# Sigmoids written as tanh, a second memory input split in place, and a new order of the side work in a two-block transformer kernel

## The chip, the cores and the metric

The kernel runs on one core of one Trainium2 chip. The metric is the device time of one execution in microseconds (us); lower is better. TensorE runs at one of two clock levels, 1.2 and 2.4 GHz; the profile prints the clock that was granted as a share of the higher one.

## The reference

512 tokens of width 1024 go through a chain of two blocks. All arrays are float32.

```python
# first block: layer A (mLSTM), then layer B (latent attention)
mem_n = rmsnorm(mem, mem_norm)                      # 256 memory tokens
mk, mv = memory_kv(mem_n, mem_w_kv[layer])          # once for each layer
# layer A
h = rmsnorm(x, norm_g)
qk, v, o, z, i_pre, f_pre, mq, mz = split_cols(h @ w_in, ...)
qk = silu(causal_conv(qk, conv_w, conv_b))
ht = rmsnorm(mlstm_chunkwise(q, k, v, i_pre + ig_b, f_pre + fg_b), h_g)
y_m = sigmoid(o) * ht * silu(z)                     # 4 heads of 256
y_mem = memory_attention(mq, mk, mv) * silu(mz)     # 4 heads of 128
x = x + concat(y_m, y_mem) @ w_out
# layer B: k, v from a latent of x, q from a latent, 8 heads of 192 with rope
y_b = chunk_causal_attention(q, k, v) * silu(z)
y_mem = memory_attention(mq, mk, mv) * silu(mz)
x = x + concat(y_b, y_mem) @ w_out
# second block, layer C
u, q, k, v, gate_logits = split(rms_norm(x, g_mix) @ w_in)
a = softmax(s[:, :, 0]) - lam * softmax(s[:, :, 1]) # differential attention, 4 heads
o = rms_norm(a @ v, g_subln) * (1 - lam_init)
mixed = concat(causal_multiscale_pool(u), o) * sigmoid(gate_logits)
x = x + mixed @ w_out
# layer D: cross attention to 256 tokens of mem_2, then the MLP
mem_n = rms_norm(mem_2, g_mem)
x = x + memory_cross_attention(rms_norm(x, g_cross), mem_n, w_cq, w_ckv, w_co)
x = x + square(relu(rms_norm(x, g_mlp) @ w_up)) @ w_down
return rms_norm(x, g_final)
```

## The kernel before

**Products.** Activations lie with features on the partitions. Each large product takes its weights in chunks of at most 512 columns by two tiles of 128 rows. A chunk is loaded (SP) into one of two raw slots, ScalarE writes its rounded high part (L1505), VectorE the low part (L1862), and TensorE adds three products, high by high, high by low and low by high (L1205 to L1207 with the activations stationary, L1210 to L1212 with the weights stationary). There are three slots for split chunks. The products are called after their outputs, in this order: mqA, mk0, mv0, mzA, then for each head of layer A qkA, ozA and vA (one for two heads), outA0 and outA1; qlB, ckvB, mk1, mv1; zB0, kvB0, quB0, mqB, kvB1, quB1, mzB0, mzB1, kvB2, quB2, zB1, kvB3, quB3, zB2, zB3, outB0, outB1; kC, qC, vC, gC4, uC, gC0, outC0, outC1; ckD0, ckD1, cqD0, cqD1, cvD0, cvD1, outD0, outD1; and up and dn of the MLP. gC4 and gC0 are the gate logits of layer C, for the attention half and for the pooling half; ckD is the keys of the cross attention, which read mem_2.

**Side work.** Everything else is cut into small steps: one score tile of an attention head (`msc`, `asc`, `dsc`, `csc`), the transposes of its probabilities (`mtp`, `atp`, `dtp`; L1168), the product with the values (`mval`, `aval`, `dval`; L1410), norms (`nsq`, `nsum`, `ndiag`, `nrow`), the gates of the mLSTM (`gateP`, `gateA`, `gateT`), the preparation of layer B's queries and keys (`prep0` to `prep6`). A unit of the differential attention is one head with one block of 128 queries: `dsc` (two score tiles, L1397, with a mask, L1184), its softmaxes, `dtp` and `dval`. At a unit's score tile VectorE takes the maximum, ScalarE the exponential, VectorE the sum's reciprocal and the scaling.

**Order.** `order_of_work()` writes one list of steps, and the program of every engine follows that list, so each engine's queue is fixed when the kernel is built. Two lanes hold side steps. After each row of a product (one tile of 128 contraction rows, L1186) `step()` takes the next group from a lane if its conditions have been put into the list and if at least `lag` ns of a planner's clock have gone by since the last group of that lane. Where a product needs a result that is still in a lane, `need()` and `force()` put the steps of the lane there one after the other, with no row of a product between them. The closing steps of the differential attention's heads (`dhs`, `dhr`, `dho`: the norm, a transpose, and the multiplication by the gate) wait in the lane for gC0's gate, and the units behind them in the same lane with them.

**ScalarE's functions.** Sigmoid and Exp belong to different table sets, and a set is loaded (ACT_TABLE_LOAD) where the function changes. SiLU is sigmoid on ScalarE (L1610) and a multiplication on VectorE (L1862); in the convolution of layer A the multiplication is GpSimd's (`csilu`, L2417).

**Memory of layer D.** mem_2 is loaded after outC0, turned (scaled by its gain and split into high and low parts) during outC1, and its norm follows after outC1. The evictions of a product that reads a normed input scale by the norm's row, so they need `nrow` first; ckD0's evictions are put behind `nrow m2`, and with it the norm's matmuls stand in TensorE's queue between the last row of ckD0 and the first of ckD1.

## Time and profile before

| what | value |
| --- | --- |
| device time, median of 3 | 1767.71 us (1767.44 to 1769.67) |
| the profiled execution's own time | 1770.57 us |
| its span in the trace | 1768.8 us |
| TensorE busy | 1649.4 us, 93% of the span |
| VectorE, ScalarE, GpSimd busy | 911.1, 730.8, 133.4 us |
| mean granted clock | 0.952 |

TensorE has little idle time in sum, so the table is read for two quantities: where its 7% of idle time lies, and where its granted clock is under 1.00. The rows by stage are further down. In the trace layer A's first head (qkA0) begins at 91.2 us, mk1 at 530.2, mzB0 at 638.2, quB2 at 695.7, zB1 at 733.7, outB0 at 837.9, kC at 928.8, gC4 at 1001.2, the last row of gC0 ends at 1079.5, outC0's first tile follows at 1106.0, outC1 begins at 1178.5, ckD0 at 1200.9, ckD1 at 1227.6 and the MLP at 1391.3.

### The profile page before, as it was taken

The numbers are of one execution on the slowest core, as the hardware profiler recorded it, in microseconds if no ns is written. First come the engines' busy times: TensorE is split into PE (matmuls) and PEld (weight loads), VectorE is DVE, ScalarE is ACT, GpSimd is POOL, SyncE is SP. The second block draws the span as 40 slices with busy tenths as digits, with TensorE's granted clock in tenths as the row PEclk, the third lists the DMA queues.
The fourth block names the chain that finished last, engine by engine and source line by source line (L and its number), as shares of the span: only waits on it lengthen the run. The fifth ranks groups of instructions, "written<-read, shape, count | busy, mean of one in ns | idle before, by whom it ended". The sixth has DMA issues, their size and how long they took to land.

```text
span 1768.8 us, 19339 instructions
## 1 busy us (share of the span) xinstructions
PE 1649.4 (93%) x7194; PEld 1276.1 (72%) x7194; DVE 911.1 (52%) x1853; ACT 730.8 (41%) x1618; POOL 133.4 (8%) x106
## 2 busy tenths in 40 slices
PE   7997999999998997888999998887999999999997
PEld 5755687777886866465678775566877788888885
DVE  6346465656466445456446556464454543434342
ACT  5534433334356566456333343343333342424241
POOL 3101010101110000000001000012000200000001
PEclk9998999999999999799999997697999999999997
DMA  5512212313324211111123221022332333333331
GB/s 173 142 48 60 60 50 82 96 52 115 113 84 121 67 43 44 32 36 60 60 84 96 84 72 59 3 85 81 105 97 73 95 95 95 96 95 96 95 96 48
DMA packets 90109, 140.99 MB, mean 80 GB/s; under 512 B 7456, under 2 KB 37536, under 8 KB 90016
## 3 DMA queue, kind: packets, MB, share of 16 engines
q1 hardware_dynamic: 89296, 139.02, 26.1%
q8 instruction: 57, 0.93, 0.2%
q10 hardware_dynamic: 720, 0.74, 0.1%
q14 instruction: 36, 0.29, 0.1%
HBM read 137.65 MB, written 2.10 MB: 79 GB/s over the span
## 4 chain that ended last, share of the span: by engine, by line
PE 73%; DVE 12%; ACT 7%; issue 4%; DMA 2%; POOL 1%; ACTq 0%; POOLq 0%; DVEq 0%; SPq 0%
PE banks L1205 15%; PE banks L1207 15%; PE banks L1206 15%; PE banks L1210 5%; PE banks L1212 5%; PE banks L1211 5%; DVE sb_arena L1862 3%; DVE sb_w_split L1862 3%; PE banks L1168 2%; DVE sb_arena L1871 2%; PE banks L1397 1%; ACT sb_w_split L1505 1%; ACT sb_junk L1473 1%; DMA sb_raw<-in_mem_w_kv 1%; ACT sb_arena L1642 1%
## 5 line engine op out<-in xcount | busy, mean ns | idle before, releaser
L1862 DVE TENSOR_TENSOR sb_w_split<-sb_raw,sb_w_split 128x512 fp32r<-128x512 f32 (+3 forms) x530 | 335.8, 676 | 363.3 <-ACT sb_w_split L1505 361.7
L1505 ACT ACTIVATE sb_w_split<-sb_raw 128x512 fp32r<-128x512 f32 (+3 forms) x530 | 287.8, 593 | 427.3 <-PE banks L1207 327.8
L1205 PE MATMUL banks<-sb_actA,sb_w_split 128*128 128x512 f32 x672 | 273.6, 407 | 2.5 <-ACT sb_arena L1560 1.1
L1207 PE MATMUL banks<-sb_actA,sb_w_split 128*128 128x512 f32 x672 | 263.4, 392 | 0.0
L1206 PE MATMUL banks<-sb_actA,sb_w_split 128*128 128x512 f32 x672 | 262.9, 391 | 0.0
L1205 PE MATMUL banks<-sb_actB,sb_w_split 128*128 128x512 f32 (+1 forms) x640 | 253.9, 397 | 7.9 <-DVE sb_actB L1862 4.4
L1206 PE MATMUL banks<-sb_actB,sb_w_split 128*128 128x512 f32 (+1 forms) x640 | 249.0, 389 | 0.0
L1207 PE MATMUL banks<-sb_actB,sb_w_split 128*128 128x512 f32 (+1 forms) x640 | 248.8, 389 | 0.0
L1210 PE MATMUL banks<-sb_w_split,sb_actA 128*128 128x512 f32 (+1 forms) x384 | 155.7, 406 | 12.9 <-DVE sb_w_split L1862 8.7
L1212 PE MATMUL banks<-sb_w_split,sb_actA 128*128 128x512 f32 (+1 forms) x384 | 150.7, 393 | 0.0
L1211 PE MATMUL banks<-sb_w_split,sb_actA 128*128 128x512 f32 (+1 forms) x384 | 150.4, 392 | 0.0
L1205 PEld LDWEIGHTS banks<-sb_actA,sb_w_split 128*128 128x128 f32 x672 | 127.1, 189 | 31.6 <-issue 5.5
L1205 PEld LDWEIGHTS banks<-sb_actB,sb_w_split 128*128 128x128 f32 x640 | 123.3, 193 | 36.3 <-issue 5.5
L1207 PEld LDWEIGHTS banks<-sb_actA,sb_w_split 128*128 128x128 f32 x672 | 126.8, 189 | 27.5
L1206 PEld LDWEIGHTS banks<-sb_actA,sb_w_split 128*128 128x128 f32 x672 | 127.2, 189 | 25.8 <-issue 1.5
L1207 PEld LDWEIGHTS banks<-sb_actB,sb_w_split 128*128 128x128 f32 x640 | 122.8, 192 | 27.1
L1206 PEld LDWEIGHTS banks<-sb_actB,sb_w_split 128*128 128x128 f32 x640 | 123.2, 192 | 26.3 <-issue 0.7
L1168 PE MATMUL banks<-sb_cons,sb_arena 128*128 128x128 f32 x460 | 83.6, 293 | 39.9 <-DVE sb_arena L1862 13.2
L2400 POOL TENSOR_TENSOR sb_arena<-sb_arena 128x512 f32<-128x512 f32 x44 | 65.4, 1488 | 716.7 <-ACT sb_arena L1546 713.9
L1168 PEld LDWEIGHTS banks<-sb_cons,sb_arena 128*128 128x128 f32 x460 | 59.1, 150 | 61.8 <-issue 17.1
L2391 POOL TENSOR_TENSOR sb_small<-sb_small,sb_cons 128x4 f32<-128x4 f32 (+3 forms) x30 | 41.7, 1389 | 785.2 <-DVE sb_small L1868 731.1
L1642 ACT ACTIVATE sb_arena<-banks,sb_small 128x256 f32<-128x256 f32 (+2 forms) x80 | 45.4, 567 | 128.9 <-DVE sb_small L1865 128.8
(176 smaller groups left out, 2167.7 us busy)
## 6 DMA issues: line engine op xcount, KB each, us to landing
sb_raw<-in_a_w_in SPq DMA_DIRECT2D x66, 256.0 KB, 3.0
sb_raw<-in_w_up SPq DMA_DIRECT2D x32, 512.0 KB, 3.7
sb_raw<-in_w_down SPq DMA_DIRECT2D x32, 512.0 KB, 3.8
sb_raw<-in_w_in SPq DMA_DIRECT2D x24, 512.0 KB, 3.6
sb_raw<-in_mem_w_kv SPq DMA_DIRECT2D x16, 512.0 KB, 3.9
sb_raw<-in_w_ckv SPq DMA_DIRECT2D x16, 512.0 KB, 3.9
sb_raw<-in_a_w_in SPq DMA_DIRECT2D x15, 512.0 KB, 3.9
sb_raw<-in_a_w_out SPq DMA_DIRECT2D x12, 512.0 KB, 3.9
```

The costliest lines, as they stand in the source:

```text
L1168: t = pe.op.transpose(v.ps[0:rows, place.bank, n * P:(n + 1) * P], block, v.ident)
L1205: pe.op.matmul(out, hi[:, cs], x.hi(k), start=i == 0, stop=False)
L1206: pe.op.matmul(out, hi[:, cs], x.lo(k), start=False, stop=False)
L1207: t = pe.op.matmul(out, lo[:, cs], x.hi(k), start=False, stop=last_i)
L1210: pe.op.matmul(out, x.hi(k)[:, cs], hi, start=i == 0, stop=False)
L1211: pe.op.matmul(out, x.hi(k)[:, cs], lo, start=False, stop=False)
L1212: t = pe.op.matmul(out, x.lo(k)[:, cs], hi, start=False, stop=last_i)
L1505: act.op.activation(hi[:, cs], raw[:, cs], ACT.Copy).then_inc(act.mark(m("w_hi"), 2 * n + part + 1), 1)
L1642: act.op.activation(prob, src, ACT.Exp, bias=v.soft("mx", step, 1), scale=scale, accum_out=v.soft("sm", step, 1)).then_inc(act.mark(empty, ...
L1862: dve.op.tensor_tensor(out, a, b, op).then_inc(dve.mark(*mark) if mark else dve.tick(), 1)
L2391: pool.op.tensor_tensor(v.stat(root, n), v.stat(mean, n), v.con("minus_half", 0, n), ALU.pow).then_inc(m.at("rstd", step)[0], 1)
L2400: pool.op.tensor_tensor(total, total, v.square_of(norm, n)[1], ALU.add).then_inc(signal, 1)
```

## The change

It does seven things.

1. Sigmoid becomes Tanh of half the argument, sigmoid(x) = (tanh(x/2) + 1)/2. The +1 goes into the multiplication that follows, which becomes a scalar_tensor_tensor (`fused`), and the factor 1/2 into constants further on. In `csilu` the multiplication by (tanh + 1) becomes two instructions of GpSimd, a multiplication and an addition. The program has 5 table loads in place of 36.
2. The ones are a constant instead of a memset by GpSimd, and `ndiag` and `nrow` are groups of their own with a lag of 2600 each, in place of one with 4500.
3. mem_2 is loaded after outB1 into places of the second activation buffer that are free then, turned in place, and its norm stands in kC and qC; between ckD0 and ckD1 there is none.
4. A row of a product is issued in parts, one for each 128-column output, and side steps may stand between the parts; a lane that is forced lets the other lane advance too.
5. The differential attention has its transposes two units behind the scores instead of one, a third buffer of probabilities, a lag of 4000 for 4600, and its closing steps wait for the gate of gC4 instead of gC0's.
6. Layer B is in another order, below.
7. In layer A `gateT` has a lag of 14000 for 4000 and the memory rounds 8000 for 4400.

```diff
@@ class Plan: force, product
             self.take(lane)
+            self.advance(1 - lane)
...
                 self.put(("mm", name, i), banks)
-                self.clock += row_ns(name)
+                for j in range(n_out(name)):
+                    self.put(("rows", name, i, j))
+                    self.clock += row_ns(name) / n_out(name)
+                    if j < n_out(name) - 1:
+                        self.advance((i * n_out(name) + j) % 2)
@@ order_of_work: scales, layer A
-            p.side(lane, (), ("ndiag", norm), ("nrow", norm), lag=4500)
+            p.side(lane, (), ("ndiag", norm), lag=2600)
+            p.side(lane, (), ("nrow", norm), lag=2600)
...
-    p.side(1, (), ("gateT",), lag=4000)
+    p.side(1, (), ("gateT",), lag=14000)
...
-           [("hnscale", "mqA"), ("silu", "mzA", 3), ("hnt", "mk0", 3)])
+           [("hnscale", "mqA"), ("silu", "mzA", 3), ("hnt", "mk0", 3)], lag=8000)
@@ layer B
     p.product("mk1")
     head_norm(0, "mk1", MT, False)
+    p.product("mqB")
+    head_norm(0, "mqB", TT, True)
     p.product("mv1")
...
-    gated("zB0")
-    p.need(("kpe",))
-    latents(0)
-    p.product("mqB")
-    mla(0)
-    head_norm(1, "mqB", TT, True)
     mem_b(0)
     mem_b(2)
-    latents(1)
     p.need(("nrow", "b"))
     gated("mzB0")
     gated("mzB1")
-    mla(2)
+    p.need(("kpe",))
+    latents(0)
+    gated("zB0")
+    for n in range(4):
+        mla(2 * n)
+    latents(1)
+    p.need(("mtp", "B", 3, 3))
+    gated("zB1")
     latents(2)
-    p.need(("mval", "B", 3))
-    gated("zB1")
-    mla(4)
-    latents(3)
     p.need(("ysplit", "yB", 1))
     gated("zB2")
+    latents(3)
     p.need(("ysplit", "yB", 3))
     gated("zB3")
-    mla(6)
@@ layer C: mem_2
     p.put(("enter", "outB1"))
+    p.put(("load_mem2",))
     p.put(("late",))
     scales(0, "c", after=[("sqp", "c", 7)])
+    for n in range(4):
+        p.soon.append(squares("m2", n) + [("turn", "m2T", 2 * n), ("turn", "m2T", 2 * n + 1)])
     p.product("kC", [("nsum", "c")])
+    scales(1, "m2", after=[("sqp", "m2", 3)])
@@ layer C: differential attention
-    for n, u in enumerate(units + [None] * 5):
+    for n in range(len(units) + 6):
...
-                after = [("gateG", "gC0")]
+                after = [("gateG", "gC4")]
...
-        if before is not None:
-            group.append(("dtp", *before))
-            turned = before
-        before = u
-        p.side(0, after, *group, lag=4600)
+        if 2 <= n < len(units) + 2:
+            turned = units[n - 2]
+            group.append(("dtp", *turned))
+        p.side(0, after, *group, lag=4000)
...
-    p.put(("load_mem2",))
-    for k in range(KD):
-        p.soon.append([("turn", "m2T", k)])
     p.product("outC1")
     p.put(("enter", "outC1"))
-    for n in range(4):
-        p.soon.append(squares("m2", n))
-    scales(1, "m2", after=[("sqp", "m2", 3)])
     scales(0, "d", after=[("sqp", "d", 7)])
-    p.product("ckD0", [("nrow", "m2")])
+    p.product("ckD0")
@@ scalar_program: silu
-            act.op.activation(sg, v.out_of(name, j), ACT.Sigmoid)...
+            act.op.activation(sg, v.out_of(name, j), ACT.Tanh, scale=0.5)...
@@ vector_program: silu
-            tensor(o, o, v.sigA[:, j % 2, :] if name == "mzA" else v.sigB[:, 0, :], ALU.mult, *m.at("silu", step))
+            fused(o, v.sigA[:, j % 2, :] if name == "mzA" else v.sigB[:, 0, :], 1.0, ALU.add, o, ALU.mult,
+                  *m.at("silu", step))
@@ gpsimd_program: csilu
-                pool.op.tensor_tensor(v.qkT[:, n, :], v.conv[:, n, :], v.u_pad[:, n, CONV_W - 1:CONV_W - 1 + SEQ],
-                                      ALU.mult).then_inc(m("qk"), 1)
+                t = v.u_pad[:, n, CONV_W - 1:CONV_W - 1 + SEQ]
+                pool.op.tensor_tensor(t, t, v.conv[:, n, :], ALU.mult).then_inc(pool.tick(), 1)
+                pool.settle()
+                pool.op.tensor_tensor(v.qkT[:, n, :], t, v.conv[:, n, :], ALU.add).then_inc(m("qk"), 1)
```

Line numbers move with the edits: the instructions of a product row are L1205 to L1207 before and L1213 to L1215 now, the score tiles L1397 and L1404, the transposes L1168 and L1176.

**TensorE's queue where gC0 ends and outC0 begins, before.** The first row is the last of gC0. Score tiles (L1397), masks (L1184), values (L1410) and transposes (L1168) of the differential attention follow, and L1420, which is a product of the pooling.

```order
L1207 MATMUL banks<-sb_actA,sb_w_split 128x512
L1420 MATMUL banks<-sb_arena 128x512 [waits dma_pool_w,pooled]
L1410 MATMUL banks<-sb_arena 128x128 [waits empty4,empty5]
L1410 MATMUL banks<-sb_arena 128x128 x3
L1397 MATMUL banks<-sb_arena 128x256 [waits empty6]
L1184 MATMUL banks<-sb_masks 128x128
L1397 MATMUL banks<-sb_arena 128x256
L1184 MATMUL banks<-sb_masks 128x128
L1168 MATMUL banks<-sb_cons,sb_arena 128x128 [waits empty5,prob]
L1410 MATMUL banks<-sb_arena 128x128 [waits empty5,empty6]
L1397 MATMUL banks<-sb_arena 128x384 [waits empty4]
L1184 MATMUL banks<-sb_masks 128x128
```

Behind these rows stand 22 more of the same kinds; only then comes the first row of outC0 (`L1205 MATMUL banks<-sb_actB,sb_w_split`). A second such stretch stands behind the first row of outC0's first tile.

**TensorE's queue in a product of layer C, now.** The place is inside one of the products gC4, uC and gC0.

```order
L1213 MATMUL banks<-sb_actA,sb_w_split 128x512 [waits empty0,w_lo]
L1214 MATMUL banks<-sb_actA,sb_w_split 128x512
L1215 MATMUL banks<-sb_actA,sb_w_split 128x512
L1417 MATMUL banks<-sb_arena 128x128 [waits empty5,empty6]
L1404 MATMUL banks<-sb_arena 128x512 [waits empty4]
L1192 MATMUL banks<-sb_masks 128x128
L1404 MATMUL banks<-sb_arena 128x512
L1192 MATMUL banks<-sb_masks 128x128
L1176 MATMUL banks<-sb_cons,sb_arena 128x128 [waits empty6,prob]
L1176 MATMUL banks<-sb_cons,sb_arena 128x128
L1213 MATMUL banks<-sb_actA,sb_w_split 128x512 [waits empty1]
L1214 MATMUL banks<-sb_actA,sb_w_split 128x512
```

The score tiles and transposes of a unit now stand between the three matmuls of one output part and those of the next.

**ScalarE's queue in layer B, before.** L1610 is the sigmoid of a gate, L1642 the exponential of a memory-attention score, L1652 and L1740 copies out of PSUM, L1505 the weight split.

```order
L1610 ACT_TABLE_LOAD [waits silu]
L1610 ACTIVATE sb_cons<-sb_arena 128x512 [waits empty0]
L1740 ACTIVATE sb_arena<-banks 128x512 [waits full7]
L1642 ACT_TABLE_LOAD [waits neg]
L1642 ACTIVATE sb_arena,sb_small<-banks,sb_small 128x256 [waits full6]
L1652 ACTIVATE sb_actB_plain<-banks 128x2x128 [waits full4]
L1740 ACTIVATE sb_arena<-banks 128x512 [waits full7]
L1505 ACTIVATE sb_w_split<-sb_raw 128x192 [waits full1,dma_raw1]
L1505 ACTIVATE sb_w_split<-sb_raw 128x192
L1610 ACT_TABLE_LOAD [waits silu]
L1610 ACTIVATE sb_cons<-sb_arena 128x512 [waits empty1]
L1642 ACT_TABLE_LOAD [waits neg]
```

**ScalarE's queue at a like place, now.** L1617 is the tanh of the gate, L1649 the exponential, L1659 the copy, L1512 the weight split.

```order
L1512 ACTIVATE sb_w_split<-sb_raw 128x384 [waits chunk,dma_raw0]
L1512 ACTIVATE sb_w_split<-sb_raw 128x384
L1649 ACTIVATE sb_arena,sb_small<-banks,sb_small 128x256 [waits neg,full4]
L1659 ACTIVATE sb_actB_plain<-banks 128x2x128 [waits full5]
L1617 ACTIVATE sb_cons<-sb_arena 128x512 [waits silu,empty0]
L1512 ACTIVATE sb_w_split<-sb_raw 128x192 [waits full1,dma_raw1]
L1512 ACTIVATE sb_w_split<-sb_raw 128x192
L1649 ACTIVATE sb_arena,sb_small<-banks,sb_small 128x256 [waits neg,full6]
L1659 ACTIVATE sb_actB_plain<-banks 128x2x128 [waits full4]
L1617 ACTIVATE sb_cons<-sb_arena 128x512 [waits silu,empty1]
L1649 ACTIVATE sb_arena,sb_small<-banks,sb_small 128x256 [waits neg,full5]
L1659 ACTIVATE sb_actB_plain<-banks 128x2x128 [waits full6]
```

The four table loads are gone; the gate's function and the exponential follow each other without one.

**TensorE's queue between ckD0 and ckD1, before.** The first row is the last of ckD0, the next three are the norm of mem_2 (L1237 sums the squares, L1246 spreads the scale over the partitions), and then comes ckD1.

```order
L1207 MATMUL banks<-sb_actB,sb_w_split 128x256
L1237 MATMUL banks<-sb_cons,sb_arena 128x1 [waits sq_sum,empty7]
L1237 MATMUL banks<-sb_cons,sb_arena 128x1 x3
L1246 MATMUL banks<-sb_arena 128x256 [waits empty7,diag,ones]
L1205 MATMUL banks<-sb_actB,sb_w_split 128x256 [waits empty0,w_lo]
```

**The same place, now.** The first row is the last of ckD0, and ckD1 follows without a norm.

```order
L1215 MATMUL banks<-sb_actB,sb_w_split 128x256
L1213 MATMUL banks<-sb_actB,sb_w_split 128x256 [waits empty0,w_lo]
L1214 MATMUL banks<-sb_actB,sb_w_split 128x256
L1215 MATMUL banks<-sb_actB,sb_w_split 128x256
```

The norm of mem_2 stands between rows of a product of layer C instead:

```order
L1220 MATMUL banks<-sb_w_split,sb_actA 128x512
L1245 MATMUL banks<-sb_cons,sb_actB_plain 128x1 [waits sq_sum]
L1245 MATMUL banks<-sb_cons,sb_actB_plain 128x1 x3
L1218 MATMUL banks<-sb_w_split,sb_actA 128x512 [waits w_lo]
```

The summing matmuls (now L1245) wait for `sq_sum`, GpSimd's sum of the squares, as before, but with product rows of layer C around them.

## Rows read from the trace of the kernel before

**Rows 1.** The page: busy time by engine, and the granted clock in 40 slices.
```profile
PE 1649.4 (93%) x7194; PEld 1276.1 (72%) x7194; DVE 911.1 (52%) x1853; ACT 730.8 (41%) x1618; POOL 133.4 (8%) x106
...
PEclk9998999999999999799999997697999999999997
```

**Rows 2.** Windows by stage: length, busy time of each engine, granted clock, DMA.
```profile
0.00:66.40 66.40, 53.02 (x211) 41.73 (x211) 37.62 (x60) 35.07 (x64) 17.79 (x22) 0.95 0.57 177
91.00:208.80 117.80, 104.57 (x396) 71.48 (x394) 62.65 (x126) 47.16 (x97) 8.77 (x5) 0.93 0.20 58
540.60:838.00 297.40, 258.56 (x1120) 188.19 (x1119) 155.43 (x414) 174.01 (x484) 19.10 (x10) 0.92 0.18 54
...
1001.20:1079.50 78.30, 76.78 (x344) 60.10 (x342) 44.64 (x101) 29.17 (x64) 0.00 (x0) 1.00 0.26 80
1079.50:1178.50 99.00, 81.28 (x285) 51.48 (x284) 48.60 (x128) 34.91 (x104) 4.03 (x4) 0.72 0.07 22
1200.90:1244.30 43.40, 31.19 (x213) 29.76 (x212) 21.46 (x43) 17.19 (x33) 12.44 (x11) 0.76 0.30 85
```

**Rows 3.** The same view, of short stretches inside those stages.
```profile
34.40:39.10 4.70, 1.17 (x4) 0.58 (x3) 3.34 (x7) 1.47 (x4) 1.41 (x2) 0.81 0.03 12
130.20:143.80 13.60, 7.83 (x25) 5.71 (x26) 10.96 (x20) 3.39 (x8) 0.00 (x0) 0.62 0.14 40
152.70:178.10 25.40, 18.23 (x65) 13.31 (x65) 13.83 (x28) 14.36 (x27) 5.87 (x4) 0.87 0.23 62
705.80:734.00 28.20, 19.36 (x50) 9.53 (x47) 11.45 (x38) 11.10 (x39) 0.00 (x0) 0.69 0.03 10
755.50:770.00 14.50, 8.06 (x31) 5.97 (x29) 8.11 (x21) 5.87 (x12) 0.00 (x0) 0.76 0.13 36
1079.50:1106.00 26.50, 19.84 (x62) 10.54 (x60) 14.01 (x38) 11.03 (x31) 1.01 (x1) 0.61 0.07 22
1110.30:1136.00 25.70, 20.50 (x63) 11.10 (x62) 12.12 (x34) 7.93 (x28) 1.01 (x1) 0.61 0.00 1
```

**Rows 4.** VectorE's timeline in one unit of the differential attention.
```profile
1027.66 0.69 DVE L2287 TENSOR_REDUCE sb_small<-banks 128x1 f32<-128x512 f32 x1
...
1031.35 0.17 DVE L2292 RECIPROCAL sb_small<-sb_small 128x2 f32<-128x2 f32 x1 [1.58 <-ACT sb_arena L1776]
...
1031.81 0.75 DVE L1871 SCALAR_TENSOR_TENSOR sb_arena<-sb_arena,sb_small 128x512 f32<-128x512 f32 x1
1032.48 0.68 DVE L1862 TENSOR_TENSOR sb_arena<-banks,sb_arena 128x512 f32<-128x512 f32 x1
```

**Rows 5.** TensorE's waits: us in total, times, longest.
```profile
PE banks L1168 <- DVE sb_arena L1862: 13.2, 4, 6.4
...
PE banks L1237 <- POOL sb_arena L2400: 9.4, 1, 9.4
...
PE banks L1210 <- ACT sb_arena L1560: 3.5, 2, 3.1
```

**Rows 6.** The page: a DMA issue, its KB and us to landing.
```profile
sb_raw<-in_w_in SPq DMA_DIRECT2D x24, 512.0 KB, 3.6
```

**Rows 7.** ScalarE by line: busy us, mean ns, idle before.
```profile
L1642 ACT ACT_TABLE_LOAD x12 | 15.4, 1283 | 34.6 <-DVE sb_small L1865 34.6
```

**Rows 8.** ScalarE's timeline round one table load: start, length.
```profile
91.05 1.28 ACT L1610 ACT_TABLE_LOAD   x1
92.34 0.63 ACT L1610 ACTIVATE sb_arena<-sb_x_res 128x512 f32<-128x512 f32 x1
```

**Rows 9.** VectorE's and GpSimd's timelines in one stretch of the convolution.
```profile
255.38 2.33 DVE L1871 SCALAR_TENSOR_TENSOR sb_arena<-sb_arena,sb_cols 128x512 f32<-128x512 f32 x3
...
258.20 4.29 DVE L1871 SCALAR_TENSOR_TENSOR sb_arena<-sb_arena,sb_cols 128x512 f32<-128x512 f32 x3
...
258.15 2.99 POOL L2417 TENSOR_TENSOR sb_arena<-sb_arena 128x512 f32<-128x512 f32 x2 [17.26 <-ACT sb_arena L1658]
```

173 lines of the change are left out of this document (95 added, 78 removed).

## The prediction

> **What bounds the kernel now.** I read the page first [rows 1]: TensorE is busy for 93% of the span and no other engine for more than 52%, so the end is set by TensorE's work plus whatever interrupts it. The strip of granted clocks says the rest: most slices are at 9, and 6 or 7 in a few places. A time over stretches therefore has two losses: idle time, and busy time at a lower clock. For a stretch of length L with busy time B and granted clock c, I count loss = (L - B) + (1 - c) B; the second part is what the same work would have saved at full clock.
>
> The windows by stage [rows 2] give these losses: 13.4 + 2.7 = 16.0 us up to 66.4; 13.2 + 7.3 = 20.5 in layer A's first head (91.0 to 208.8); 38.8 + 20.7 = 59.5 from mk1 to the end of layer B's attention (540.6 to 838.0); 1.5 + 0 in gC4, uC and gC0; 17.7 + 22.8 = 40.5 in outC0 and the stretch ahead of it (1079.5 to 1178.5); 12.2 + 7.5 = 19.7 round ckD0 (1200.9 to 1244.3). Together 156.2 us. The matmuls themselves are not made fewer by the change, so a gain has to come out of these 156.2 us.
>
> Inside the stages I looked for knots [rows 3]. Loss by the same formula: 3.8 (34.4), 8.8 (130.2), 9.5 (152.7), 14.8 (705.8), 8.4 (755.5), 14.4 (1079.5), 13.2 (1110.3). In the last two, TensorE executes some 62 instructions in 26 us, at 0.61 of the clock, with VectorE busy for half of the time: score, softmax and transpose follow each other, nobody has other work to put between. The reader is to see there the forced steps that the queue listings show: no product rows, so each engine waits for the other. The granted clock is 1.00 in the 78 us before, with 98% busy, and falls where TensorE comes to be busy for 75% (19.84 of 26.5).
>
> **The change, part by part.**
>
> *Layer C (28 us).* The closing steps wait for gC4's gate instead of gC0's, so the lane is no longer blocked through uC and gC0, and the units of the two forced stretches go between product rows. Is there room? The work moved is 19.84 x 0.61 + 20.50 x 0.61 = 24.6 us of TensorE at full clock and 14.0 + 12.1 = 26.1 us of VectorE [rows 3]. gC4 to gC0 now have 44.6 us of VectorE in 78.3 [rows 2]; with the moved work it is 70.8 in 102.9, or 69%. So it fits on average. The latency of one unit is 1032.56 - 1027.66 = 4.9 us from the first maximum to the scaled probabilities [rows 4], and with the transposes two units behind the scores, at least one product row stands between. I take both forced losses as gone, 14.4 + 13.2 = 27.6, and leave the other 12.9 us of the 40.5. Bounds: 41 (all of it), and 12 if the in-order queue of VectorE paces each unit (below).
>
> *Layer B (40 us).* Of 59.5 us, the block of forced memory-attention steps between quB2 and zB1 is 14.8 [rows 3], and it goes: the memory units come earlier, beside mzB0 to zB0. What stays, by my count: mk1 is now followed by mqB, whose first row waits for the same ScalarE copies, 3.1 of the 3.5 us [rows 5]; two of the four waits for `prep6` (L1168 behind L1862, 13.2 in total, longest 6.4 [rows 5]) remain forced, at the ends of zB0 and zB2, since latents(1) and the queries of the last heads need them: 2 x 6 = 12; and gaps of about 5 us where softmaxes pace. That is 20, so 59.5 - 20 = 39.5. Bounds: 20, if only the forced block (14.8) and a little of the rest (5) goes; 60, if all goes. VectorE has 155.4 us of work in 297.4, 52% [rows 2], so it has the room.
>
> *Layer A (14 us).* 20.5 us of loss, of which 8.8 lie at 130.2 (the gates of the mLSTM, forced, at 0.62 of the clock) and 9.5 at 152.7 [rows 3]. The memory rounds with a lag of 8000 leave room in VectorE's queue, and the gate chain starts earlier relative to the convolutions. I take the first entirely and half of the second: 8.8 + 4.8 = 13.6. Bounds 5 and 20.
>
> *Start (4.5 us).* `nrow a` moves into mqA instead of following it, which is the knot at 34.4 [rows 3]: 3.8; with no memset to wait for, some 0.7 more. The loads of the first weights stay. Bounds 0 and 7.
>
> *Entry of layer D (14 us).* The norm of mem_2 no longer stands between ckD0 and ckD1. It ended a wait of 9.4 us for GpSimd [rows 5], and the stretch's low clock (7.5 of the 19.7) came with it. Where the stall goes: in kC and qC the same sum by GpSimd has product rows round it, and nobody needs the row before ckD0's evictions. What is late next I can't read off a row; I leave the other 5.7 us of the stretch in place. mem_2's two loads now stand in SP's queue ahead of weights of kC; a chunk of w_in lands 3.6 us after its issue [rows 6], so the delay lies between 0 and 3.6, and I take 0, as the raw slots are filled ahead. Bounds 8 and 18.
>
> *Tanh.* 31 table loads of 1283 ns leave ScalarE, 39.8 us [rows 7]. ScalarE isn't the bound, so that is worth nothing by itself; only the 12 loads ahead of an exponential (15.4 us) stand in the chain score, maximum, exponential, transpose. Where TensorE waits for that chain they are inside the losses above, and I add nothing; if they came on top, 15.4 more. The next ACTIVATE starts 0.01 us after a load ends [rows 8]. The Trainium skill (ScalarE: Activation LUTs, What ACT_TABLE_LOAD costs) puts a drain of about 1380 ns on top of each load; this row shows none, and by the page that upper bound would be 12 x 2.66 = 32 us. The fused form costs 0.75 us for 0.68 [rows 4], for some fifty instructions 4 us of VectorE, hidden under product rows.
>
> *The convolution's second GpSimd instruction (costs 4 us).* 16 more instructions of 1.49 us (2.99 for two) [rows 9], 24 us of GpSimd, which is idle otherwise. But three fused operations of VectorE take 2.33 us alone and 4.29 us beside 2.99 us of GpSimd's: 0.65 us lost for each us. So 24 x 0.65 = 15.6 us of VectorE at most, in layer A, where its share is 53% [rows 2]; a quarter on the path is 4. Bounds 0 and 15.6. The Trainium skill (SBUF — State Buffer, Who interferes with whom) says that a VectorE instruction with two SBUF inputs and a GpSimd instruction that reads SBUF exclude each other for their whole length; that speaks against this edit, and by it the bound would be 24 us and not 15.6. The row shows a delay of two thirds.
>
> **Sum.** 28 + 40 + 14 + 4.5 + 14 - 4 = 96.5 us. The profiled execution took 1770.6 us (1.8 over its span) and is 2.9 over the median of 1767.7. So 1770.6 - 96.5 - 2.9 = 1671.
>
> **The rivals.** A measurement of this kernel can tell about 0.2% (3.5 us) from no change.
>
> *Main case*, all as summed: 1671, own range 1652 to 1690, chance 0.55.
>
> *VectorE's queue paces (0.20).* The queue is in order, so a unit's maximum may stand behind a weight split that waits for ScalarE, and the next weights' split behind the unit's reciprocal. For: in the unit shown, 1.6 of 4.9 us are one wait for ScalarE's exponential [rows 4]. Against: the full clock in gC4 to gC0 with units already between rows [rows 2]. Then layer B gives 20 and layer C 12: 1671 + 20 + 16 = 1707.
>
> *Nothing left (0.14).* The split of product rows lets every unit hide, B gives 60 and C 41: 1671 - 20 - 13 = 1638. For: VectorE's 52% and 69%. Against: the prep6 waits are forced still.
>
> *GpSimd's lock on the path (0.05).* All 15.6 us: 1671 + 11 = 1682.
>
> *The clock stays low (0.06), the other side.* If spread units make TensorE as little busy in gC4 to gC0 as in the forced stretch (75% busy, clock 0.61), a us of product work takes 1 / (0.75 x 0.61) = 2.19 us, 1.19 more. With C's 28 lost, 68.5 us of gain are left, and 68.5 / 1.19 = 58 us of the 78 decide: beyond, the kernel is slower. For all 78: 1671 + 28 + 93 = 1792; for half, 1745. For: spread work makes small gaps everywhere, where now they are in two places. Against: from 540.6 to 838.0, with units all through and 87% busy, the mean was still 0.92 [rows 2].
>
> **How the numbers follow.** The range 1640 to 1708 runs from the case with nothing left to that of VectorE's queue; outside lie the low clock (0.06), half of the best case and a tail of the queue's, 0.18 in all. Faster by over 0.2%: 0.94. Slower: 0.05, the low clock over 58 us. Within: 0.01.
>
> **What would show it.** In the new trace: no stretch without product rows near 1010 us and 990 us of the new span (the old 1079 and 1110), and the clock strip at 9 there; layer B's loss near 20, with two waits of L1176 for VectorE of 5 to 6 us; no wait of TensorE for GpSimd at ckD1; 5 table loads; VectorE's convolution rows longer beside GpSimd's. The prediction is wrong if the forced stretches turn into many waits of 0.5 to 2 us for VectorE or ScalarE in B and C, or if the clock strip shows more than four slices under 9.

## The result and the profile after

The changed kernel takes 1716.7 us (median of 4, 1714.8 to 1722.0) against 1767.7 us: ratio 0.971, 95% interval 0.969 to 0.974. It is faster, but by 51 us, about half of the 96.5 that the prediction had, and it lies 9 us outside the predicted range. The profiled execution took 1714.8 us, its span is 1713.0.

The page of the changed kernel, its engines and its strip of granted clocks (answers to [rows 1]):

```profile
PE 1611.0 (94%) x7194; PEld 1258.9 (73%) x7194; DVE 921.0 (54%) x1856; ACT 691.6 (40%) x1587; POOL 149.6 (9%) x115
...
PEclk9998999999999999999999999899999999999998
```

The slices at 7 and 6 are gone, and three slices are under 9, fewer than the prediction's sign of being wrong (more than four). In this respect the mechanism came out as forecast. Where the time came from is to be read by stage. The windows of the changed kernel, cut at the first rows of qkA0, qkA1, mk1, outB0, kC, gC4, outC1, ckD0, cqD0, up00 and dn31 (columns as in [rows 2]: length, busy time of each engine, clock, DMA):

```profile
89.20:190.80 101.60, 95.71 (x368) 67.17 (x369) 58.07 (x108) 34.10 (x71) 12.31 (x9) 0.95 0.22 63
190.80:411.70 220.90, 213.45 (x949) 163.75 (x947) 137.08 (x264) 68.47 (x146) 34.19 (x27) 1.00 0.21 63
524.20:818.20 294.00, 259.03 (x1161) 191.31 (x1161) 161.16 (x426) 164.23 (x497) 20.11 (x11) 0.97 0.20 60
818.20:905.60 87.40, 85.46 (x372) 64.14 (x373) 42.99 (x84) 32.90 (x68) 4.26 (x3) 1.00 0.23 76
905.60:983.40 77.80, 73.37 (x341) 59.27 (x340) 53.15 (x109) 32.07 (x60) 12.01 (x9) 1.00 0.34 102
983.40:1144.30 160.90, 147.25 (x626) 105.20 (x625) 93.52 (x228) 59.44 (x163) 4.03 (x4) 0.94 0.18 53
1166.00:1196.40 30.40, 26.76 (x204) 25.89 (x204) 21.02 (x35) 13.60 (x24) 7.42 (x5) 0.94 0.39 123
1342.40:1670.60 328.20, 328.20 (x1451) 271.55 (x1450) 147.13 (x223) 114.77 (x193) 7.45 (x5) 1.00 0.31 97
```

The kernel before, cut at the same products, where [rows 2] had other cuts:

```profile
208.80:415.60 206.80, 205.96 (x926) 160.53 (x924) 128.53 (x250) 73.14 (x141) 21.53 (x15) 1.00 0.24 69
530.20:837.90 307.70, 268.67 (x1161) 195.90 (x1161) 162.16 (x430) 182.44 (x511) 20.11 (x11) 0.92 0.19 56
837.90:928.80 90.90, 87.95 (x372) 64.95 (x373) 42.78 (x80) 34.17 (x69) 4.26 (x3) 1.00 0.24 76
928.80:1001.20 72.40, 71.56 (x332) 58.17 (x330) 45.89 (x97) 26.27 (x46) 7.44 (x6) 1.00 0.33 95
1001.20:1178.50 177.30, 158.06 (x627) 111.57 (x625) 93.24 (x228) 64.07 (x167) 4.03 (x4) 0.85 0.16 48
...
1391.30:1724.70 333.40, 333.13 (x1451) 271.30 (x1450) 147.23 (x223) 114.71 (x193) 7.60 (x6) 1.00 0.32 95
```

| stretch | before | after | saved | forecast |
| --- | --- | --- | --- | --- |
| mqA to qkA0 | 83.3 | 80.6 | 2.7 | 4.5 |
| layer A, head 0 (qkA0 to qkA1) | 117.6 | 101.6 | 16.0 | 14, less 4 for GpSimd |
| layer A, heads 1 to 3 | 206.8 | 220.9 | -14.1 | 0 |
| mk1 to outB0 | 307.7 | 294.0 | 13.7 | 40 |
| outB0 to kC | 90.9 | 87.4 | 3.5 | 0 |
| kC to gC4 | 72.4 | 77.8 | -5.4 | 0 |
| gC4 to outC1 | 177.3 | 160.9 | 16.4 | 28 |
| ckD0 to cqD0 | 43.4 | 30.4 | 13.0 | 14 |
| up00 to dn31 (MLP) | 333.4 | 328.2 | 5.2 | 0 |

The lengths are differences of the starts of the products in the two traces. The rows add up to 51.0 us; the stretches between them that are left out give 3.8 more, and the start and the end 1.0. So the traces lie 55.8 us apart, 5 more than the medians: the profiled execution of the kernel before was slower than its median, and that of the changed kernel faster. Four lines have a forecast of 0 and moved all the same: heads 1 to 3, outB0 to kC, kC to gC4, and the MLP, in which no step was changed.

By loss (idle plus the share of busy time that the clock took), mk1 to outB0 went from 39.0 + 21.5 to 35.0 + 7.8 us, and gC4 to outC1 from 19.2 + 23.7 to 13.7 + 8.8. (The latter is the place of both forced stretches.) So in layer B only 4.0 us of idle time went, and 13.7 came from the clock, less 4 us that TensorE's work (busy time by clock) grew. The prediction had layer B's loss near 20 us; it is 42.8. TensorE's waits in the changed kernel, for mk1 to outB0 (us in total, times, longest):

```profile
PE banks L1218 <- DVE sb_arena L1875: 6.6, 2, 4.7
PE banks L1176 <- DVE sb_arena L1875: 5.7, 4, 3.5
PE banks L1176 <- ACT sb_arena L1750: 4.4, 2, 3.4
PE banks L1213 <- DVE sb_arena L1875: 4.1, 2, 2.4
PE banks L1218 <- ACT sb_arena L1567: 3.6, 2, 3.2
PE banks L1218 <- ACT sb_arena L1591: 3.0, 2, 1.5
```

L1213 and L1218 are the first matmuls of product rows, L1176 is a transpose. The prediction kept two waits of L1176 for VectorE, of 6 us each; there are four, 5.7 us together. The rows of L1213 and L1218 are waits of a product's first row for work of VectorE or ScalarE, and only one of them (L1567, 3.2 us behind mk1) was in its count.

In the stretch from gC4 to outC1 the other sign of being wrong did show: the forced stretches turned in part into 8 waits of 0.5 to 2 us, 11.3 us together. Before there were 6 such waits, 7.8 us, beside 5 longer ones of 12.1 us.

### The profile page after: what moved, and what is told of

Its sections match the earlier page's. It is cut to its first block, busy times and chain, and to the rows that moved or that the text cites. A ratio compares the mean times of both kernels' runs of the same rounds, so it can differ in the third digit from the quotient of the medians.

```text
span 1713.0 us, 19330 instructions
## 1 busy us (share of the span) xinstructions
PE 1611.0 (94%) x7194; PEld 1258.9 (73%) x7194; DVE 921.0 (54%) x1856; ACT 691.6 (40%) x1587; POOL 149.6 (9%) x115
## 3 DMA queue, kind: packets, MB, share of 16 engines
q1 hardware_dynamic: 89296, 139.02, 26.7%
## 4 chain that ended last, share of the span: by engine, by line
PE 71%; DVE 15%; ACT 7%; issue 4%; DMA 3%; POOL 0%; SPq 0%; ACTq 0%; DVEq 0%; POOLq 0%
PE banks L1213 15%; PE banks L1215 15%; PE banks L1214 15%; PE banks L1218 4%; PE banks L1220 4%; PE banks L1219 4%; DVE sb_w_split L1875 4%; DVE sb_arena L1875 3%; DVE sb_arena L1884 3%; PE banks L1176 2%; ACT sb_junk L1480 2%; ACT sb_w_split L1512 1%; PE banks L1336 1%; DVE sb_arena L1878 1%; PE banks L1404 1%
## 5 line engine op out<-in xcount | busy, mean ns | idle before, releaser
L1875 DVE TENSOR_TENSOR sb_w_split<-sb_raw,sb_w_split 128x512 fp32r<-128x512 f32 (+4 forms) x530 | 342.0, 687 | 368.2 <-ACT sb_w_split L1512 367.1
L1512 ACT ACTIVATE sb_w_split<-sb_raw 128x512 fp32r<-128x512 f32 (+4 forms) x530 | 288.0, 593 | 439.1 <-PE banks L1215 323.5
L1213 PE MATMUL banks<-sb_actA,sb_w_split 128*128 128x512 f32 x672 | 279.4, 416 | 6.6 <-ACT sb_arena L1567 2.3
L1215 PE MATMUL banks<-sb_actA,sb_w_split 128*128 128x512 f32 x672 | 264.7, 394 | 0.0
L1214 PE MATMUL banks<-sb_actA,sb_w_split 128*128 128x512 f32 x672 | 264.5, 394 | 0.0
L1213 PE MATMUL banks<-sb_actB,sb_w_split 128*128 128x512 f32 (+1 forms) x640 | 249.0, 389 | 8.5 <-DVE sb_arena L1875 3.9
L1215 PE MATMUL banks<-sb_actB,sb_w_split 128*128 128x512 f32 (+1 forms) x640 | 243.7, 381 | 0.0
L1214 PE MATMUL banks<-sb_actB,sb_w_split 128*128 128x512 f32 (+1 forms) x640 | 243.6, 381 | 0.0
L1218 PE MATMUL banks<-sb_w_split,sb_actA 128*128 128x512 f32 (+1 forms) x384 | 156.1, 406 | 23.8 <-DVE sb_w_split L1875 9.1
L1213 PEld LDWEIGHTS banks<-sb_actA,sb_w_split 128*128 128x128 f32 x672 | 128.1, 191 | 37.8 <-issue 11.6
L1215 PEld LDWEIGHTS banks<-sb_actA,sb_w_split 128*128 128x128 f32 x672 | 127.7, 190 | 28.1
L1213 PEld LDWEIGHTS banks<-sb_actB,sb_w_split 128*128 128x128 f32 x640 | 121.4, 190 | 34.2 <-issue 10.7
L1214 PEld LDWEIGHTS banks<-sb_actB,sb_w_split 128*128 128x128 f32 x640 | 121.5, 190 | 23.1 <-issue 1.4
L1215 PEld LDWEIGHTS banks<-sb_actB,sb_w_split 128*128 128x128 f32 x640 | 121.4, 190 | 22.9
L2423 POOL TENSOR_TENSOR sb_arena<-sb_arena 128x512 f32<-128x512 f32 x41 | 61.6, 1501 | 705.9 <-ACT sb_arena L1553 703.3
L1649 ACT ACTIVATE sb_arena<-banks,sb_small 128x256 f32<-128x256 f32 (+2 forms) x80 | 45.4, 568 | 169.0 <-DVE sb_small L1878 169.0
L1218 PEld LDWEIGHTS banks<-sb_w_split,sb_actA 128*128 128x128 f32 x384 | 74.1, 193 | 41.2 <-issue 16.0
L1176 PE MATMUL banks<-sb_cons,sb_arena 128*128 128x128 f32 x460 | 80.8, 285 | 24.8 <-DVE sb_arena L1875 11.4
```

The costliest lines, as they stand in the source:

```text
L1176: t = pe.op.transpose(v.ps[0:rows, place.bank, n * P:(n + 1) * P], block, v.ident)
L1213: pe.op.matmul(out, hi[:, cs], x.hi(k), start=i == 0, stop=False)
L1214: pe.op.matmul(out, hi[:, cs], x.lo(k), start=False, stop=False)
L1215: t = pe.op.matmul(out, lo[:, cs], x.hi(k), start=False, stop=last_i)
L1218: pe.op.matmul(out, x.hi(k)[:, cs], hi, start=i == 0, stop=False)
L1512: act.op.activation(hi[:, cs], raw[:, cs], ACT.Copy).then_inc(act.mark(m("w_hi"), 2 * n + part + 1), 1)
```

## The experiments

All are compared with runs of the kernel before on the same chip, whose median lay between 1766.6 and 1767.2 us. Where a stretch is compared with the changed kernel's, its scatter has to be known: the same instructions took between 290.7 and 294.4 us from mk1 to outB0, between 158.0 and 164.9 from gC4 to outC1 and between 77.8 and 81.5 from kC to gC4 in the profiles of kernels whose code there is identical. Much of this goes with the granted clock (below). The experiments are spread over four chips, and where one is compared with another on a different chip (12, 14 and 17 with 11), a difference of a few us is weaker than its digits look.

**1. The place of actB.** The changed kernel also allocates the second activation buffer, actB, right behind actA, which the list of the change doesn't name. Here it goes back behind the other buffers:

```diff
         sb("actA", [P, 2, KD, SEQ], F32R)
-        with nc.sbuf_tensor("sb_actB", [P, 2, 12, SEQ], F32R) as both:
-            mem["actB"] = both
-        sb("actB_plain", [P, 2, 12, SEQ])
...
         sb("junk", [P, 512])
+        with nc.sbuf_tensor("sb_actB", [P, 2, 12, SEQ], F32R) as both:
+            mem["actB"] = both
+        sb("actB_plain", [P, 2, 12, SEQ])
```

> The changed kernel with one edit: the second activation buffer (actB) is allocated last again, as before, instead of right behind actA; orders, functions and steps stay. In the changed kernel each product that reads actB takes 21.8 us where it took 22.4, and those of 12 rows 32.6 where they took 33.6, and no step of theirs was changed. Theory one, the place of the buffer sets the length of its matmuls: the MLP goes back from 350.2 to 356 us, outA1 and outB1 to 33.6, and the kernel loses about 12 us, to some 1729. Rival, the place is nothing and the shorter products come from the new order of loads and splits: the time stays at 1717 within 3 us.

Measured: 1716.2 us (1711.8 to 1722.0), ratio 0.972 (0.969 to 0.974), and the MLP (up00 to dn31) 328.3 us. Theory one fell as it stood, and the rival's number held; its explanation did not, as the next two show.

**2. The same move in the kernel before.**

> The kernel before with that edit alone, the other way: actB allocated right behind actA. Theory one: the MLP falls from 356 to 350 us and the kernel from 1768 to about 1756. Rival: 1768 within 3 us.

Measured: 1757.3 us, ratio 0.995 (0.993 to 0.997): 9.4 us faster, as theory one had it. The windows from mk1 to outB0 and, further on, of the MLP:

```profile
526.60:831.40 304.80, 266.17 (x1160) 194.56 (x1161) 161.75 (x430) 182.42 (x511) 20.11 (x11) 0.93 0.20 57
...
1383.10:1711.80 328.70, 328.43 (x1451) 271.44 (x1450) 147.04 (x223) 114.68 (x193) 7.61 (x6) 1.00 0.32 96
```

So the place does count in the kernel before and not in the changed one. What differs is where actB begins when it stands last: the changed kernel's constants are 816 columns wide (the 128 columns of ones) against 689. So in the changed kernel actB begins at a multiple of 128 bytes in either place.

**3. Only the start of actB in the kernel before.**

```diff
-CONSTS = [..., ("minus_half", 16), ("ones", 1)]
+CONSTS = [..., ("minus_half", 16), ("ones", 1), ("spare", 15)]
```

> The kernel before with 15 unused columns added to its constants, and nothing else: every buffer that is allocated behind them moves up, and the second activation buffer (actB) begins at a multiple of 64 bytes instead of 32 bytes past one. Putting actB back behind the others in the changed kernel left its products at 21.8 us, and there too it begins at a multiple of 64 bytes, since the changed kernel's constants are wider. Theory one, that start is what counts: each product that reads actB falls from 22.4 to 21.8 us, the MLP from 356 to 350 and the kernel from 1767 to 1755 to 1758, as with actB moved forward. Rival, the neighbour or the bank of memory counts: 1767 within 3 us.

Measured: 1760.0 us, ratio 0.995 (0.993 to 0.997), 6.6 us faster, with no instruction changed. The MLP's window:

```profile
1385.00:1715.40 330.40, 330.13 (x1451) 271.53 (x1450) 147.22 (x223) 114.77 (x193) 7.60 (x6) 1.00 0.32 96
```

That is between the two others: 333.4, 330.4, 328.7. By the buffers' sizes, each rounded up to 32 bytes, actB begins 32, 64 and 0 bytes past a multiple of 128. The time falls short of theory one's 1755 to 1758. The products say the same as the windows: in the MLP each two down products, which read actB (192 matmuls), take 44.8, 44.0 and 43.5 us in these three, and the products of the same length that read actA take 43.5 or 43.6 in all of them. Between experiment 2 and the kernel before, actB alone changes its remainder, and experiment 1 shows that its place is nothing otherwise; a multiple of 128 is best of the three. The middle value is less sure: in experiment 3 the arena and the other buffers behind the constants move by 32 bytes too.

**4. The arena's start in the changed kernel** (one spare column; the arena then begins at a multiple of 128 bytes instead of 96 past one).

> The changed kernel with one unused column more in its constants, so that the arena, which holds nearly all of the small buffers, begins at a multiple of 128 bytes instead of 32 bytes before one, as it did in the kernel before; actB keeps its place. Theory one, as for actB, TensorE reads the arena's operands faster: matmuls on the arena are some 1000 of 7194 at about 7 ns each, so 3 to 8 us less, to about 1711. Rival, only operands of large products show it and the arena's place is nothing: 1717 within 3 us.

Measured: 1719.8 us (1711.4 to 1724.4), ratio 0.974 (0.972 to 0.977). No gain: the rival holds, though the four runs lie 13 us apart. The effect is seen for actB's products only.

**5. Sigmoid back in the changed kernel.**

```diff
-ACT.Tanh
+ACT.Sigmoid
```

> The changed kernel with Sigmoid in place of Tanh in every such ScalarE instruction, all else the same (the output is not the reference's, since the arithmetic round it is still that for tanh). It brings back 36 table loads, 41 in place of 5, and nothing else. Theory one, ScalarE has slack and only loads ahead of an exponential or an eviction on which TensorE waits count: 36 loads of 1.28 us are 46 us of ScalarE, and the kernel loses 5 to 15 us, to 1722 to 1732. Rival, the loads were worth nearly all that the change brought: the kernel loses 30 to 46 us, to about 1750 to 1763. Second rival, nothing: within 3 us of 1717.

Measured: 1740.5 us, ratio 0.985 (0.984 to 0.987), 24 us slower than the changed kernel. That is above theory one's 5 to 15 and below the rival's 30: neither number held. Its windows for head 0 and for mk1 to outB0:

```profile
87.50:196.40 108.90, 95.66 (x370) 67.13 (x370) 57.66 (x108) 42.69 (x78) 12.29 (x9) 0.92 0.20 58
...
535.80:841.50 305.70, 263.81 (x1160) 194.04 (x1160) 160.61 (x426) 184.70 (x513) 20.12 (x11) 0.94 0.20 57
```

In the second, ScalarE has 20.5 us more (184.7 for 164.2) and the stretch is 11.7 us longer, though ScalarE is busy for 60% of it. Layer A's heads 0 to 3 together are 13.3 us longer.

**6. Tanh in the kernel before**, the same edit the other way (the output is not the reference's).

> The kernel before with Tanh in place of Sigmoid as the function of each such ScalarE instruction and no other edit (its argument isn't halved and nothing is added, so the output is not the reference's): 5 table loads instead of 36, in the old order. Theory one, the loads cost about as much in the old order as in the new one, where putting them back cost 24 us: 1767 falls to 1740 to 1748. Rival, the old order's forced stretches hide or repeat the loads differently: under 12 us of gain, over 1755. Second rival, all of the change's gain but the place of actB: under 1735.

Measured: 1755.5 us, ratio 0.993 (0.992 to 0.995), 11.1 us faster, which is the rival's number (the two profiled executions lie 16 us apart). Its window from mk1 to outB0:

```profile
527.70:822.00 294.30, 260.96 (x1161) 192.09 (x1161) 162.45 (x430) 164.47 (x497) 20.11 (x11) 0.94 0.20 59
```

294.3 us, in the old order, with the forced block still in it (26.5 us without a product row): the table loads alone bring all that the whole change brought there (294.0). Of the 13.4 us, 5.7 are idle time and 5.8 the clock. The loads are worth 11 us in the old order and 24 in the new one; the rest of the difference lies mostly in layer A (3.1 us there in the old order, 13.3 in the new). Experiments 2 and 5 say the same from the other side: with sigmoid the stretch takes 304.8 us in the old order with actB moved, and 305.7 in the new one.

**7. Layer B in the old order, all else changed.**

> The changed kernel with layer B in the old order of products and lanes (zB0, kvB0, quB0, mqB and so on, and the forced memory-attention steps between quB2 and zB1), all other edits kept, tanh among them. With Sigmoid in place of Tanh the new layer B took 305.7 us against 307.7 in the kernel before, with tanh 294.0. Theory one, the new order is worth little and the tables carried layer B's gain: the stretch from mk1 to outB0 stays at 294 within 5 us and the kernel at 1717 within 6. Rival, as predicted, the order is worth the 14.8 us of the forced block and more: 15 to 30 us slower.

Measured: 1715.9 us, ratio 0.971 (0.969 to 0.973). The windows from mk1 to outB0 and on to kC:

```profile
527.30:821.20 293.90, 260.85 (x1168) 192.03 (x1169) 163.49 (x432) 164.82 (x499) 20.10 (x11) 0.96 0.20 59
821.20:906.10 84.90, 84.26 (x364) 63.60 (x365) 41.38 (x78) 31.96 (x66) 4.26 (x3) 1.00 0.25 81
```

Theory one holds: the new order is worth nothing. The forced block is still there, without a product row, and costs 9.5 us of idle time and 2.8 by the clock:

```profile
707.40:728.90 21.50, 11.99 (x37) 5.91 (x36) 6.84 (x24) 12.74 (x47) 1.64 (x1) 0.77 0.05 13
```

In the new order the longest stretch without a product row is 8.9 us, and yet idle time from mk1 to outB0 is 35.0 us without the block and 33.0 with it. The old order here has the old lag of the memory rounds (2400 ns for 2800) and the old condition ahead of kvB3 as well.

**8. and 9. Less work for VectorE or for ScalarE in layer B.** VectorE's edit; ScalarE's puts the same two lines ahead of its own part of the split.

```diff
+                if name in SHORT:
+                    cs = slice(part * half, part * half + 64)
```

> The changed kernel with VectorE's part of the weight split cut to 64 columns of each half in layer B's products (mk1 to zB3), so that it leaves out most of the low parts there (the output is not the reference's); each such instruction goes from about 0.7 to about 0.2 us, and some 120 of them save 50 to 60 of VectorE's 161 us in the 294 us of the stretch. Theory one, VectorE's queue is late there, since evictions and softmax steps stand behind splits: the stretch falls by 10 us or more, the kernel to 1707 or less. Rival, what is left are latencies of chains over several engines and forced steps, which VectorE's load does not change: under 5 us.

> The changed kernel with ScalarE's part of the weight split cut to 64 columns of each half in layer B's products (most of the high parts are left out, so the output is not the reference's); some 120 instructions fall from 0.6 to about 0.2 us and save some 45 to 50 of ScalarE's 164 us in the stretch of 294. The same cut on VectorE gave 6.2 us there. Theory one, ScalarE's queue is what lets TensorE wait in layer B, as the table loads (11 to 15 us of its time, 12 to 13 us of the stretch) say: the stretch falls by 12 us or more, the kernel to 1705 or less. Rival, the rest are chains of latencies and forced steps: under 6 us.

Measured: 1714.0 us (ratio 0.970, 0.968 to 0.972) with VectorE's splits cut, 1717.7 us (0.972, 0.970 to 0.975) with ScalarE's. The windows from mk1 to outB0, first VectorE's cut:

```profile
526.40:814.20 287.80, 256.47 (x1160) 190.30 (x1160) 138.56 (x425) 164.09 (x497) 20.10 (x11) 0.97 0.21 61
```

then ScalarE's:

```profile
525.00:813.90 288.90, 256.78 (x1163) 190.16 (x1161) 160.94 (x426) 143.91 (x497) 20.10 (x11) 0.97 0.21 61
```

VectorE's cut takes 22.6 us off VectorE, ScalarE's 20.3 off ScalarE (under half of what was expected of either), and the stretch falls by some 2 to 6 us from its 290.7 to 294.4. Idle time stays at 31.3 and 32.1. The rivals hold: the weight splits of either engine are a small part of what TensorE waits for. In the changed kernel's stretch TensorE waits once for a split:

```profile
PE banks L1218 <- DVE sb_w_split L1875: 0.2, 1, 0.2
```

That 20 us of table loads were worth 12 and 20 us of splits about 4 is no contradiction: a split is mostly done ahead, while the load in front of an exponential itself waits for the softmax's maximum ([rows 7]: ScalarE idles ahead of it). So ScalarE doesn't use its idle time for the load, and each of those stands whole in the chain. This reading is argued from the queue and the waits; no run moved the loads alone to other places.

**10. Side steps between whole rows only, everywhere.**

```diff
-                    if j < n_out(name) - 1:
-                        self.advance((i * n_out(name) + j) % 2)
```

> The changed kernel with no side step between the parts of a product row, so that side steps stand only between whole rows, as before (three matmuls for each of the outputs, then side steps); all other edits stay. Theory one, finer places for side steps gain a few us of waits and cost TensorE about as much in exposed weight loads (its work, busy time by clock, is 4 us more in layer B and 4 in layer C than before): within 5 us of 1717. Rival, the fine places carry the gain of layers B and C: 15 us or more slower, to over 1730. Second rival, they cost more than they bring: under 1712.

Measured: 1719.0 us, ratio 0.972 (0.971 to 0.974), as theory one had it. The windows from mk1 to outB0, outB0 to kC and, further on, gC4 to outC1:

```profile
523.50:804.60 281.10, 248.69 (x1123) 186.20 (x1124) 157.37 (x414) 158.70 (x485) 20.10 (x11) 0.96 0.22 63
804.60:917.10 112.50, 102.79 (x410) 73.29 (x411) 48.18 (x96) 37.76 (x80) 4.25 (x3) 0.92 0.18 57
...
992.10:1145.90 153.80, 144.42 (x628) 105.72 (x627) 92.33 (x228) 58.90 (x163) 4.40 (x4) 0.94 0.18 55
```

Layer B moves work into outB0 and loses 12 us in the two stretches together (393.6 us for 381.4); layer C gains 7, and kC to gC4 2.8. The small sum hides two effects of opposite sign. The old order with whole rows and tanh took 385.3 us in the same two stretches (experiment 6), so the new order seems to need the finer places only to break even.

**11. Whole rows from kC on only.**

```diff
-                    if j < n_out(name) - 1:
+                    if j < n_out(name) - 1 and self.fine:
...
     p.put(("enter", "outB1"))
+    p.fine = False
```

> The changed kernel with side steps between the parts of a product row up to outB1 only, and from kC on between whole rows. Without them anywhere, layers C's stretch (kC to outC1) fell from 238.7 to 228.8 us, and the stretch from mk1 to kC rose from 381.4 to 393.6. Theory one, these are two separate effects: the kernel gains 8 to 10 us, to about 1708. Rival, layer C's 10 us are noise of the clock or of how layer B leaves off: within 3 us of 1717.

Measured: 1706.7 us (1703.6 to 1706.9), ratio 0.965 (0.964 to 0.967). It is the fastest kernel of the study, 10 us faster than the changed one, as theory one had it. The window from gC4 to outC1:

```profile
982.10:1133.60 151.50, 141.02 (x626) 102.19 (x625) 92.10 (x228) 58.86 (x163) 4.40 (x4) 0.98 0.19 56
```

TensorE's work is the same (138 us by the clock). Idle time is 10.5 us and the clock 0.98, against 13.7 us and 0.94, so 3 of the 9.4 us are idle time and 6 the clock. The stretch took 151.1, 152.0 and 150.0 us in experiments 14, 17 and 18, which share nearly all of this code.

**12. A lag of 5200 for layer C's units on top of that.**

> The last but one kernel's edit (whole rows from kC on) with a lag of 5200 instead of 4000 for the units of the differential attention, which puts 5, 6 and 5 units into gC4, uC and gC0 instead of 6, 8 and 2. In the run with whole rows uC took 67.5 us and gC0 23.3. Theory one, uC is overfull: its units follow each other faster than their chain over VectorE and ScalarE, and spreading them gains 5 to 12 us more, to 1695 to 1702. Rival, each unit costs the same wherever it stands: 1707 within 3 us.

Measured: 1711.0 us, ratio 0.969 (0.967 to 0.971), and gC4 to outC1 158.7 us. Theory one fell: spreading the units over three products costs 7 us in the stretch and 4 in the median, so an overfull uC is not what is left. The rival's 1707 within 3 did not hold either.

**13. The closing steps behind gC0's gate again.**

```diff
-                after = [("gateG", "gC4")]
+                after = [("gateG", "gC0")]
```

> The changed kernel with the closing steps of the differential attention waiting for gC0's gate again instead of gC4's, so that its lane is blocked through uC and gC0 and 10 units of 16 come at or behind the end of gC0; the depth of two and the third probability buffer stay. Theory one, the gate is the edit that carries layer C's gain: the stretch gC4 to outC1, 160.9 us, goes up by 12 to 20 us, and the kernel to 1729 to 1737. Rival, the depth of two and finer places carry it, and the forced stretches cost little now: under 6 us.

Measured: 1728.4 us, ratio 0.978 (0.976 to 0.979), 11.7 us slower than the changed kernel. The window from gC4 to outC1:

```profile
983.60:1156.80 173.20, 158.26 (x625) 111.05 (x624) 94.34 (x228) 59.78 (x163) 4.03 (x4) 0.85 0.16 49
```

The clock is back at 0.85 as before, and a stretch of 26.7 us without a product row is back too. Theory one holds: this one line is 12 of the 16 us of layer C. The depth of two, the third buffer and the lag were not tried alone.

**14. mem_2's steps one product and a half later, on top of 11.**

> The kernel with whole rows from kC on (1706.7 us), with the squares and turns of mem_2 in vC instead of kC and its norm in vC and gC4 instead of qC. Theory one, in kC and qC these steps delay the evictions and rotations of k and q and cost 3 to 5 us there, which vC has room for: kC to gC4 falls from 75.1 to 72.5 to 73, the kernel by 2 us or more. Rival, they cost the same in vC: within 2 us.

Measured: 1712.5 us (1707.0 to 1712.9), ratio 0.969 (0.967 to 0.971); kC to gC4 80.4 us. That is 6 us slower than experiment 11, where neither expectation had it. In experiment 11 kC to gC4 took 75.1 us, so whole rows alone bring 2.7 of the 5.4 us back that the changed kernel lost there. That the rest are mem_2's steps is argued from the rows (the changed kernel against the one before: VectorE 53.2 us for 45.9, TensorE's idle time 4.4 for 0.8), not shown.

**15. Layer A's lags as before.**

> The changed kernel with layer A's lags as before: 4000 for the gates' transpose and 4400 for the memory-attention rounds instead of 14000 and 8000. In the changed kernel head 0 (qkA0 to qkA1) is 16.0 us shorter than before and heads 1 to 3 are 14.1 us longer. Theory one, the lags only move memory-attention units from head 0 to heads 1 and 2, and the sum is what it was: head 0 goes back up by 8 to 12 us, heads 1 to 3 down by as much, the kernel stays at 1717 within 4 us. Rival, the lags are what brought head 0's gain and GpSimd's second instruction is what cost heads 1 to 3: head 0 goes up by 8 to 12 and heads 1 to 3 stay, so that the kernel is 8 us or more slower.

Measured: 1721.3 us, ratio 0.975 (0.973 to 0.977). The windows of head 0 and of heads 1 to 3:

```profile
87.50:207.70 120.20, 106.97 (x410) 73.16 (x410) 67.15 (x139) 39.91 (x90) 12.26 (x9) 0.94 0.18 53
207.70:416.30 208.60, 204.88 (x908) 159.23 (x907) 129.38 (x234) 62.71 (x125) 33.93 (x27) 0.99 0.22 66
```

Head 0 is 18.6 us longer and heads 1 to 3 are 12.3 shorter: the lags move memory-attention units from the one to the other, and their net worth is 6 us there and 4.6 in the median. That is theory one's mechanism, with larger shifts than it had.

These rows also split layer A's small gain. Head 0 to head 3 took 324.4 us before, 321.3 with tanh alone (experiment 6), 328.8 here and 322.5 in the changed kernel: 3.1 us saved by tanh, 7.5 lost by the other edits, of which GpSimd's second instruction is the one that experiment 16 tries, and 6.3 saved by the lags.

**16. One GpSimd instruction for each tile.**

```diff
-                pool.op.tensor_tensor(t, t, v.conv[:, n, :], ALU.mult).then_inc(pool.tick(), 1)
-                pool.settle()
-                pool.op.tensor_tensor(v.qkT[:, n, :], t, v.conv[:, n, :], ALU.add).then_inc(m("qk"), 1)
+                pool.op.tensor_tensor(v.qkT[:, n, :], t, v.conv[:, n, :], ALU.mult).then_inc(m("qk"), 1)
```

> The changed kernel with one GpSimd instruction for each tile of the convolution's gate instead of two: the addition is left out (so the output is not the reference's), 16 instructions of 1.5 us less. In the changed kernel layer A's heads 1 to 3 (190.8 to 411.7) take 220.9 us where they took 206.8. Theory one, GpSimd's second instruction delays VectorE, and VectorE's late evictions let TensorE wait at the heads' products: that stretch falls by 5 to 12 us. Rival, the stretch is longer only because memory-attention units were moved into it (TensorE's own work there is 7.4 us more): it falls by less than 2 us.

Measured: 1707.5 us, ratio 0.967 (0.965 to 0.968), 9 us less than the changed kernel. The windows of head 0 and of heads 1 to 3:

```profile
89.20:188.50 99.30, 93.18 (x368) 64.99 (x369) 56.51 (x108) 34.07 (x71) 7.25 (x5) 0.98 0.22 64
188.50:404.30 215.80, 212.71 (x949) 163.63 (x947) 131.62 (x269) 70.26 (x149) 18.45 (x15) 1.00 0.23 67
```

GpSimd has 20.8 us less in the two, VectorE 7.0 us less, TensorE's idle time is 4.1 us less, and the two stretches together are 7.4 us shorter (up to 10 against other runs with the same code there). Theory one's cost is there, at its lower end (5.1 us in heads 1 to 3): the second instruction costs 7 to 9 us. Whether it reaches TensorE through VectorE's delays or through a later end of the gate itself isn't separated by this run.

**17. The gate on VectorE, on top of 11.**

```diff
@@ order of layer A
-        p.need(("gateT",))
+        p.need(("csilu", h), ("gateT",))
...
         p.product(f"ozA{h}")
...
@@ vector_program
+        elif kind == "cgate":
+            h = a[0]
+            for n in (2 * a[1], 2 * a[1] + 1):
+                dve.wait_ge(m("csig"), 4 * h + n + 1)
+                if h:
+                    dve.wait_ge(*m.full(("hsc", h - 1, TT - 1), 1))
+                fused(v.qkT[:, n, :], v.u_pad[:, n, CONV_W - 1:CONV_W - 1 + SEQ], 1.0, ALU.add, v.conv[:, n, :],
+                      ALU.mult, m("qk"), 4 * h + n + 1)
```

> The kernel with whole rows from kC on (1706.7 us), with the convolution's gate, (tanh + 1) times the convolution, as one fused instruction of VectorE for each tile in place of GpSimd's two, two tiles to a step of the following product. VectorE gets 16 instructions of 0.75 us, 12 us, and GpSimd loses 32 of 1.5 us, 48 us, beside which VectorE's instructions were delayed by 0.65 us for each us, up to 31. Theory one, the contention costs layer A more than the fused instruction: the stretch qkA0 to outA0, 325.5 us, falls by 5 to 12 us and the kernel to 1695 to 1702. Rival, VectorE in its order now waits for ScalarE's tanh and for TensorE, which GpSimd did aside: 1707 or slower.

The gates of a head are put behind `csilu` as steps of ozA. `csilu` now holds ScalarE's four tanhs of the head, and its GpSimd part is gone.

Measured: 1716.5 us, ratio 0.972 (0.970 to 0.973), 10 us slower than 11. The window of heads 1 to 3, and TensorE's first waits in it:

```profile
190.60:422.10 231.50, 217.69 (x948) 167.58 (x947) 132.15 (x282) 72.12 (x151) 3.02 (x3) 0.97 0.22 64
```

```profile
PE banks L1220 <- DVE sb_w_split L1877: 9.1, 3, 4.4
```

VectorE has 5 us less to do than in the changed kernel, and the stretch is 8.3 us longer than in 11 (223.2), because TensorE waits 9.1 us for weight splits that it waited for in none of these heads there. The rival's number holds, its reason does not. Two waits of 4.38 us make 8.8 of the 9.1; here is the first, in the order of ScalarE, VectorE and TensorE:

```profile
316.59 0.63 ACT L1667 ACTIVATE sb_arena<-sb_arena 128x512 f32<-128x512 f32 x1 [2.18 <-DVE sb_arena L1886]
317.12 2.17 ACT L1514 ACTIVATE sb_w_split<-sb_raw 128x512 fp32r<-128x512 f32 x4
317.77 1.29 DVE L1877 TENSOR_TENSOR sb_w_split<-sb_raw,sb_w_split 128x512 fp32r<-128x512 f32 x2 [1.21 <-ACT sb_w_split L1514]
319.12 0.80 PE L1220 MATMUL banks<-sb_w_split,sb_actA 128*128 128x512 f32 x1 [4.38 <-DVE sb_w_split L1877]
```

ScalarE's tanh (L1667) waits for the convolution on VectorE, ScalarE's split stands behind the tanh, VectorE's split behind that, and TensorE's first row of ozA behind both. The gate itself stands behind the splits in VectorE's queue. What puts the tanhs there is the edit of the order, which needs `csilu` ahead of ozA and not behind it. So this run doesn't price the gate on VectorE; a kernel with the gate there and the tanhs where they were wasn't run.

**18. Layer B's old order on top of 17.**

> That kernel with layer B in the old order. Theory one, the order is worth nothing here too: within 4 us of the kernel with the gate on VectorE, a little faster rather than slower (it was 0.8 us faster in the first comparison). Rival, the first comparison was chance: 8 us or more apart.

Measured: 1709.4 us (1709.0 to 1712.0), ratio 0.968 (0.967 to 0.969), 7 us faster than 17. mk1 to outB0 takes 293.1 us (291.1 in 17) and outB0 to kC 84.9 (87.4): the two stretches say that the order is worth nothing, as in 7; the median is between the two expectations, and no stretch of the two traces explains it. The old order isn't slower in either comparison. Experiment 11 with the old order and GpSimd's gate wasn't run.

## Why the prediction was wrong

**What bounds the kernel, and the loss as idle time plus clock: right.** All gains but one came out of those stretches. The exception is the start of actB, which the sum did not know: about 9 us (1766.7 to 1757.3 in experiment 2), of which 4.7 are in the MLP. The count of the losses also left out its own 1.5 us in gC4 to gC0, which changes nothing. "The matmuls themselves are not made fewer" was true, but those on actB became shorter.

**Layer B, 40 us: wrong, the largest miss.** 13.7 us came, and experiment 6 gets 13.4 of them without any reordering. The step that failed is "the block of forced memory-attention steps between quB2 and zB1 is 14.8, and it goes", together with "gaps of about 5 us where softmaxes pace". The block went, and most of the idle time of the stretch stayed: 39.0 us before, 33.0 in the old order with all else changed, 35.0 in the new order. The waits moved to the first rows of products and to other transposes (the rows above). The removed stall was counted as a gain, and its next place was bounded by a guess of 5 us and not by rows. The 20 us that were to stay were idle time alone, so all 20.7 us of the clock's loss were taken as gone, where 7.8 stayed (the clock rose from 0.92 to 0.97).

**Tanh, "I add nothing": wrong.** It is worth 11 us in the old order and 24 in the new. "ScalarE isn't the bound" rests on busy shares (41%), which do not say whether TensorE waits for a chain with a load in it. The prediction had that chain, priced it at 15.4 us, and put it inside the losses of layers A and B, which it then gave to the reordering. The price by the row, 1283 ns a load, was right: 14 to 16 loads are 18 to 20 us of ScalarE in layer B. Its "only the 12 loads ahead of an exponential" was too narrow: that row is of the memory attention's exponential alone, and five more loads stand ahead of exponentials elsewhere (L1669 of the mLSTM and L1776 of the differential attention).

**Layer C, 28 us: the mechanism right, the size wrong.** Both forced stretches went, the strip shows it, and experiment 13 shows that the gate's line is what did it (12 us). 16.4 came. The step that failed is "I take both forced losses as gone" in a kernel that also puts side steps between the parts of a row: that edit, for which the sum had no cost, takes 9.4 of the missing 11.6 us (experiment 11: 151.5 us instead of 160.9). With whole rows the gain is 25.8 us, near the 27.6 of the sum. TensorE waits in gC4 and uC 10.7 us in 9 places for ScalarE's copy of the transposed probabilities, in the changed kernel (L1417 is the product with the values):

```profile
PE banks L1417 <- ACT sb_arena L1801: 10.7, 9, 1.9
```

Why whole rows do better there isn't settled. A larger lag, which also spaces the units, does not help (experiment 12).

**Layer A, 14 us: head 0 gave 16.0, and heads 1 to 3 took 14.1 back.** The step that failed is that the longer lag "leaves room": it moves work of the memory attention out of head 0 (6 us of TensorE's) into heads 1 to 3 (7.5 us more there), which had 0.8 us of idle time before, and experiment 15 turns that back. The lags are worth 6.3 us and not 13.6; with tanh's 3.1 and the 7.5 of the other edits net 1.9 us were left.

**GpSimd, 4 us: under-sized, inside its bounds.** It costs 7 to 9 (experiment 16). The rival with all of it on the path (15.6) was too high. VectorE lost 7.0 us for 20.8 of GpSimd, 0.34 for each us and not 0.65, and the stretches lost 7.4 us, as much as all of that, not a quarter. One reason for the 0.34 lies in the timelines: the instructions of GpSimd that multiply or add tiles lie beside VectorE's with two inputs in SBUF for 31.9 us in the changed kernel and 20.2 with one instruction, so only some 12 of the 20.8 us overlap (an estimate, as the timelines merge neighbours). The Trainium skill (SBUF — State Buffer, Who interferes with whom) says that such a pair locks each other out for a whole instruction. Of the 12 us VectorE lost 7.0, or six tenths, near the 0.65 of the row that the prediction used. Its 24 us took all of GpSimd's time as overlapping.

**Layer D, 14 us: right**, 13.0 here (the stretch took 29.9 to 32.5 us in the runs with the same code), and TensorE's wait for GpSimd between ckD0 and ckD1 is gone. No run undoes this edit alone. "Nobody needs the row" may have overlooked what stands beside it: kC to gC4 grew by 5.4 us, of which whole rows take 2.7 back.

**Start, 4.5:** 4.5 came up to mzA, and 1.9 went again in mzA.

**The rivals.** "VectorE's queue paces" gave 1707, 10 us off and nearest. That is luck in good part. Less load on VectorE gave some 3 to 6 us in layer B (experiment 8), layer C's missing us came from the finer places, and heads 1 to 3 and the MLP weren't in its sum. Where a queue did cost 8 us (17), it was ScalarE's, and what the queue waited for counted, not how much was in it. The clock did not stay low.

**The range** was too narrow at the upper end for a reason that can be named: the terms of layers A, B and C were bounded one by one, and the case in which removed stalls come back was taken for B and C alone (a chance of 0.20, 36 us), with no term for layer A, where work moved into a stretch that was full.

## What to carry to other kernels

A forced block of side work is a visible loss, but its removal is worth only the part of its chains that something hides, and here that was 16 of 28 us in layer C and nothing in layer B; count the stall again at its next place before calling it a gain. A table load, or any instruction ahead of a chain's link, is to be priced by the chain that waits and not by the engine's busy share. An experiment that moves one instruction to another engine may have to move its neighbours in the order, and then it measures those (17). Edits that look like one ("finer places for side steps") can have opposite signs in two stages: compare by stage, and keep the one that pays, which here made 1706.7 us of 1716.7.

## What the runs showed of the hardware

Where a buffer begins changes the time of matmuls that read it. The same MLP took 333.4, 330.4 and 328.7 us with actB (by the sizes of the buffers ahead of it) 32, 64 and 0 bytes past a multiple of 128, and each two of its down products (192 matmuls) 44.8, 44.0 and 43.5 us. No such effect of the arena's start was seen (experiment 4).

The granted clock isn't the same for the same instructions. In kC to gC4 TensorE had 73.4 us of work in both kernels; the changed kernel got 1.00 and took 77.8 us, the kernel with one GpSimd instruction, whose code there is identical, got 0.96:

```profile
896.40:977.90 81.50, 76.54 (x341) 61.67 (x340) 53.15 (x109) 32.04 (x60) 12.01 (x9) 0.96 0.33 98
```

The four runs of the changed kernel lie 7 us apart, those of experiment 4 13 us and those of experiment 11 3 us, so a difference of 3 us in one stretch of one profile says nothing by itself.
